# Moving part of an input projection and a compress chain beside attention units

## The reference

```python
mod = c @ w_ada[l] + b_ada[l]                    # six vectors of 1024
h = rms_norm(x, g_pre_mix[l]) * (1.0 + sc1[:, None]) + sh1[:, None]
proj = h @ w_in[l]                               # q_n, kc, vc, ks, vs, kw, vw, gates, q_d, k_d, v_d, qi, ki, wi
o_nsa = nsa_attention(rope(q_n), rope(kc), vc, rope(ksl), vsl, rope(kw), vw, ...)
o_dsa = dsa_attention(rope(q_d), rope(k_d), v_d, rope(qi), rope(ki), wi)
o = jnp.concatenate([o_nsa, o_dsa], axis=-1) @ w_out[l]
```

## Time and profile before

| what | us |
|---|---|
| median of 3 runs (lowest, highest) | 1342.13 (1339.54, 1344.83) |
| the profiled execution | 1338.55 |
| its span, first to last instruction | 1336.7 |
| first projection product | 25.75 |
| last projection product starts | 95.78 |
| scores of unit 0, 7 and 16 start | 100.23, 143.58, 185.76 |
| the heads' outputs are transposed | 222.75 |

### The profile page before, as it was taken

One profiled execution on the slowest core, in us unless ns is written; L12 is line 12 of the kernel. 1 busy time (PEld: TensorE's weight loads), 2 busy tenths in 40 slices (PEclk: granted clock), 3 DMA queues, 4 the chain that ended last, 5 costly groups with the idle time before them and its releaser, 6 DMA issues.

```text
span 1336.7 us, 13883 instructions
## 1 busy us (share of the span) xinstructions
PE 1147.5 (86%) x4788; PEld 748.5 (56%) x4788; DVE 846.1 (63%) x1810; ACT 478.0 (36%) x1042; POOL 555.8 (42%) x479
## 2 busy tenths in 40 slices
PE   6699899899999989999757797878978988877877
PEld 3577667699978689876623353433424434323332
DVE  5673578545453478665686767767677766777553
ACT  3453324556544566655212222122221222222211
POOL 2463632476676555413153343333433333334330
PEclk8896589999999999999978998888988889888998
DMA  9461243645476543222299999999999999999994
GB/s 386 188 215 37 91 143 114 248 158 183 164 272 225 177 146 127 95 79 95 90 423 422 420 422 421 422 420 422 420 422 421 421 421 421 422 421 421 422 421 167
DMA packets 53462, 381.15 MB, mean 285 GB/s; under 512 B 6160, under 2 KB 6544, under 8 KB 7568
## 3 DMA queue, kind: packets, MB, share of 16 engines
q0 software_dynamic: 36864, 268.45, 48.3%
q1 hardware_dynamic: 15664, 111.00, 23.0%
q10 hardware_dynamic: 864, 0.82, 0.2%
HBM read 379.20 MB, written 1.05 MB: 284 GB/s over the span
## 4 chain that ended last, share of the span: by engine, by line
PE 47%; DMA 33%; DVE 13%; ACT 3%; issue 3%; POOL 1%; PEldq 0%; PEld 0%; SPq 0%; DVEq 0%; POOLq 0%; ACTq 0%
DMA arena<-uv_dram,arena 22%; PE bank L766 14%; PE bank L1427 11%; PE row_bank L766 8%; PE bank L730 7%; DMA ring<-uv_dram,arena 5%; PE row_bank L730 3%; DMA ada<-uv_dram,arena 2%; DMA mix_rows<-uv_dram,arena 2%; DVE gain_rows_in L2767 2%; PE bank L1405 2%; POOL v_lo L1974 1%; DVE arena L2192 1%; PE bank L894 1%; DVE arena L2655 1%
## 5 line engine op out<-in xcount | busy, mean ns | idle before, releaser
L1427 PE MATMUL bank<-arena 128*128 128x512 f32 x684 | 338.3, 646 | 96.6 <-ACT arena L1895 96.2
L1974 POOL TENSOR_TENSOR v_lo<-ring,d_hi 128x512 fp32r<-128x512 f32 x189 | 267.1, 1427 | 260.6 <-ACT d_hi L1528 201.6
L1427 PEld LDWEIGHTS bank<-arena 128*128 128x128 f32 x684 | 137.8, 206 | 281.3 <-issue 161.5
L1962 POOL DMA_INDIRECT arena<-uv_dram,arena x171 | 161.5, 945 | 304.1 <-PE bank L1427 266.9
L1528 ACT CAST d_hi<-ring 128x512 fp32r<-128x512 f32 x204 | 123.5, 619 | 143.9 <-PE bank L766 85.6
L2767 DVE SCALAR_TENSOR_TENSOR gain_rows_in<-arena,row_bank 128x1024 f32<-128x1024 f32 x86 | 104.9, 1220 | 81.1 <-DMA arena<-uv_dram,arena 81.1
L1887 ACT ACTIVATE arena<-arena 128x4 f32<-128x4 f32 x64 | 13.1, 205 | 393.0 <-DVE gain_rows_in L2767 393.0
L2054 DVE TENSOR_TENSOR v_lo<-ring,d_hi 128x512 fp32r<-128x512 f32 x63 | 56.5, 897 | 140.1 <-ACT d_hi L1528 132.3
L2767 DVE SCALAR_TENSOR_TENSOR arena<-arena,row_bank 128x1024 f32<-128x1024 f32 x85 | 103.7, 1220 | 47.8 <-DMA arena<-uv_dram,arena 47.6
L1895 ACT ACTIVATE arena<-ident,arena 128x128 f32<-128x128 f32 x256 | 81.7, 389 | 108.3 <-DVE arena L2774 108.1
L730 PE MATMUL bank<-arena 128*128 128x128 f32 (+6 forms) x456 | 74.4, 320 | 9.5 <-DVE arena L2258 3.7
(11 more groups left out here) (390 smaller groups left out, 2270.1 us busy)
## 6 DMA issues: line engine op xcount, KB each, us to landing
ring<-w_dram SPq DMA_DIRECT2D x93, 1024.0 KB, 4.9
arena<-w_dram SPq DMA_DIRECT2D x9, 1024.0 KB, 11.2
arena<-uv_dram,arena POOLq DMA_INDIRECT x171, 24.2
x<-x_dram SPq DMA_DIRECT2D x1, 1024.0 KB, 5.5
arena<-mem_dram SPq DMA_DIRECT2D x1, 1024.0 KB, 17.5
out_dram<-x SPq DMA_DIRECT2D x2, 512.0 KB, 4.9
arena<-const_dram SPq DMA_DIRECT2D x1, 868.0 KB, 18.1
ring<-uv_dram,arena POOLq DMA_INDIRECT x34, 24.7
```

Of the source, the lines that this page charges most:

```text
L1427: last = nc.tensor.matmul(acc[tb, c][:, :], diag[:, s % N_DIAG, :], expert_rows(s)[:, D + c * 512:D + (c + 1) * 512], start=False, stop=(s ...
L1962: nc.gpsimd.indirect_dma_start(expert_rows(s), None, uv_in, bass.IndirectOffsetOnAxis(ap=ids[:, s:s + 1], axis=0)).then_inc(s_got[s % ROWS ...
L1974: nc.gpsimd.tensor_tensor(v_lo[:, r, :], dense_quarter(d, r), d_hi[:, r, :], ALU.subtract).then_inc(s_dpl, 1)
```

## The change

- Tile order: group 1 of `w_in` comes last (after 4), the two compress tiles come after the modulation tiles of 4 and 5 instead of before.
- Head: PE multiplies groups 0, 2, 3 (first halves), 0, 2, 3 (second halves), then 4. ACT splits ("in", 0, 1) ahead of the wait for the second gain, and the tile after it ahead of the memory's norm. DVE weighs both halves of early tile 3 before it splits the second tile. Group 1 is multiplied in PE's loops 1 to 4 (a quarter each) and 5 and 6 (two each); DVE rotates it in loops 7 and 8; its two `pairT` groups come in loop 9.
- All four index score products stand in loop 0 (before: loops 1 and 2). The compress chain moves from loops 0, 3, 4, 6, 7, 12, 13 to 12, 13, 14, 16, 17, 20, 21. The memory's transposes move from loops 20 to 23 to 24 and 25, their last two copies on DVE behind the units.
- `FILLED` goes from 11 loops to 18 (7 to 24); `WEIGH_UNITS`, `ROUNDS_AT`, `MOD_AT`, banks and some scratch buffers change.

```diff
-    tiles = [("in", n, k) for k in range(2) for n in range(3)]
-    tiles += [("in", n, k) for n in range(3, 5) for k in range(2)]
+    tiles = [("in", n, k) for k in range(2) for n in (0, 2, 3)]
+    tiles += [("in", n, k) for n in (4, 1) for k in range(2)]
+    tiles += [("ada", n, k) for k in range(2) for n in (4, 5)]
     tiles += [("cmp1", n, 0) for n in range(2)]
-    tiles += [("ada", n + m, k) for n in (4, 6) for k in range(2) for m in range(2)]
+    tiles += [("ada", n, k) for k in range(2) for n in (6, 7)]
...
-MOD_AT = {13: 5, 14: 4, 19: 6, 23: 7, 24: 8}
-WEIGH_UNITS = [2, 2, 5, 6, 7, 10, 11, 12, 12, 13, 13, 14, 15, 16, 16, 17, 17, 18, 19, 20, 20, 21, 21, 22]
+MOD_AT = {13: 4, 15: 5, 18: 6, 23: 7, 24: 8}
+WEIGH_UNITS = [0, 3, 4, 5, 6, 9, 9, 11, 11, 14, 14, 15, 15, 16, 16, 16, 20, 20, 20, 21, 21, 21, 22, 23]
...
-FILLED = (8, 9, 10, 11, 14, 15, 16, 17, 18, 19, 24)
-PAIR_GROUPS = ((0, 2), (5, 3), (1, 4), (6, 5), (4, 6), (2, 7), (3, 1))
-BESIDE = {0: ((("kcT",), 6), (("vcT",), 7)), 1: ((("L", 0), 6), (("L", 1), 7)), 2: ((("L", 2), 6), (("L", 3), 7)),
...
+FILLED = (0, *range(7, 25))
+PAIR_GROUPS = ((0, 0), (5, 1), (1, 2), (6, 3), (4, 6))
+BESIDE = {0: tuple((("L", n), (4, 5, 2, 3)[n]) for n in range(4)), 1: ((("in", 1, 0), 6), (("in", 1, 1), 7)),
+          9: ((("pairT", 2), 6), (("pairT", 3), 7)), 12: ((("kcT",), 4), (("vcT",), 5)),
+          13: ((("cmp", 0), 4),), 14: ((("cmp", 1), 5),), 16: ((("kcmp",), 4), (("vblk",), 5)),
+          17: ((("Sc", 0), 4), (("Sc", 1), 5)), 20: ((("pcT",), 6),), 21: ((("Oc", 0), 7), (("Oc", 1), 6)),
+          24: ((("memT", 0), 0), (("memT", 1), 1)), 25: ((("memT", 2), 6), (("memT", 3), 7))}
...
+                if 1 <= i < 5:
+                    in_quarter(1, 0, i - 1)
+                if i == 5 or i == 6:
+                    in_quarter(1, 1, 2 * (i - 5))
+                    in_quarter(1, 1, 2 * (i - 5) + 1)
+                if i == 9:
+                    pe.wait_ge(s_rot, 2)
+                    pair_features(2)
+                    pair_features(3)
+                if i == 12:
+                    compress_rows("kcT", rot, ROT_KC * HD)
+                    compress_rows("vcT", plain, PL_VC)
+                if i == 13 or i == 14:
+                    compress(i - 13)
...
             for q in range(2):
                 h1_high(q)
-            high_parts(("in", 2, 0))
+            high_parts(("in", 0, 1))
             act.wait_ge(s_gain, 2)
             for q in range(2, 4):
                 wait_read(act, ("h1T", q))
                 h1_high(q)
+            high_parts(("in", 2, 1))
             act.wait_ge(s_mem, 16)
             root(1, tmp)
...
             weigh_early(3, 0)
-            low_parts(("in", 1, 0))
             weigh_early(3, 1)
+            low_parts(("in", 2, 0))
             weigh_early(1, 0)
-            low_parts(("in", 2, 0))
+            low_parts(("in", 3, 0))
             weigh_early(1, 1)
...
+                j = i + 2
+                if j == 0:
+                    low_parts(("in", 1, 0))
...
+                if j == 5:
+                    low_parts(("in", 1, 1))
+                if j == 7:
+                    rotated(1, 0)
+                if j == 8:
+                    rotated(1, 1)
+                    nc.vector.memset(coef[:, 0:1], 0.0).then_inc(s_rot, 1)
+                if j == 12 or j == 13:
+                    compress_copied(j - 12)
```

More of the change, by code:

```diff
@@ L186, in psum_plan @@
     for tb in range(TB):
-        group(("in", 3, tb), 4 + tb)
-    for tb in range(TB):
-        group(("in", 4, tb), tb)
+        group(("in", 4, tb), 4 + tb)
     for n, bank in PAIR_GROUPS:
@@ L936, in _ @@
                 in_quarter(0, 0, r)
-            for n in range(1, 3):
+            for n in (2, 3):
                 for r in range(4):
@@ L941, in _, with pair_features @@
             ada_columns(1)
-            for n in range(3):
+            for n in (0, 2, 3):
                 for r in range(4):
                     in_quarter(n, 1, r)
[L945 to L948, removed]
+            for half in range(2):
+                for r in range(4):
+                    in_quarter(4, half, r)
             pe.wait_ge(s_const, 1)
             pe.wait_ge(s_rot, 1)
-            for n, _ in PAIR_GROUPS:
+            def pair_features(n):
                 ps = begin(("pairT", n))
@@ L964, in _ @@
                 end(last, ("pairT", n))
+            for n, _ in PAIR_GROUPS:
+                pair_features(n)
             def compress_rows(which, src, first):
@@ L1609, in _, with last_quarter @@
                 free(ins, ("pairT", n))
+            for n, _ in PAIR_GROUPS:
+                pair_copied(n)
+            high_parts(("in", 1, 0))
+            def last_quarter(r):
+                d = DENSE_AT[("in", 1, 1)]
+                wait_loaded(act, ("in", 1, 1))
+                act.wait_ge(s_dused, 4 * d + r - 3)
+                nc.scalar.copy(d_hi[:, r, :], dense_quarter(d, r)).then_inc(s_dhi, 1)
+                if r == 3:
+                    highs[0] += 1
             def hidden(which):
@@ L1630, in beside1 @@
             def beside1(i):
[L1632 to L1638, removed]
+                if i == 0:
+                    for n in range(4):
+                        index_relu(n)
+                if 2 <= i < 6:
+                    last_quarter(i - 2)
+                if i == 9:
+                    pair_copied(2)
+                    pair_copied(3)
@@ L1648, in beside1 @@
                     ps = wait_full(act, ("pcT",))
                     free(nc.scalar.copy(pcT.rearrange("p b t -> p (b t)"), ps[:, 0:T]), ("pcT",))
[L1650 to L1657, removed]
+                if i == 22:
+                    high_parts(("out", 0, 0))
@@ L1659, in _ @@
+                if i == 24:
+                    for q in range(2):
+                        ps = wait_full(act, ("memT", q))
+                        for kk in range(2):
+                            k = 2 * q + kk
+                            ins = nc.scalar.activation(memT[:, k, :], ps[:, kk * T:(kk + 1) * T], ACT.Copy,
+                                                       scale=vcol("memg", k))
+                        free(ins, ("memT", q))
             attention(UNITS1, lambda u, tb: KINDS[u[0]] + tb * HEADS + u[1], [(0, P), (P, P + T)], beside1)
-            wait_full(act, ("PT", *UNITS1[-1]))
@@ L2428, in _ @@
             low_parts(("out", 0, 0))
+            for q in range(2, 4):
+                ps = wait_full(dve, ("memT", q))
+                for kk in range(2):
+                    k = 2 * q + kk
+                    ins = ts(memT[:, k, :], ps[:, kk * T:(kk + 1) * T], vcol("memg", k), None, ALU.mult)
+                free(ins, ("memT", q))
             tt(gg[:, 0:8], mod[:, 16:24], vall("g_post_mix"), ALU.mult).then_inc(s_ggf, 1)
```

121 lines of the change are left out of this document (51 added, 70 removed).

## The result

| | median us (lowest, highest) | runs |
|---|---|---|
| before | 1341.31 (1339.03, 1344.83) | 5 |
| after | 1352.90 (1350.15, 1353.11) | 5 |

The ratio is 1.0072, with a 95% interval of 1.0057 to 1.0087: the change makes the kernel 11.6 us slower. 1328.5 was forecast, and 1339 was the upper end of the range.

A forecast was written before the change was run, and what follows sets the result against it. PE's order, with its low clock, was taken to bound the first 230 us. Terms -16.5 - 12.7 + 12.4 + 2.8 + 0.4 = -13.6 gave 1325.0 profiled, median 1328.5; range for 8 of 10: 1313 to 1339.

The forecast's parts named there:

- half of it at 0.5 costs +10 (4 to 20): Loops 12 to 15, behind the hole: half of about 20 us of full-clock work runs at half clock, +10 us.
- a low spell after the mask's wait or in unit 17: +3 (0 to 8): Unit 16 to the outputs' transposes: a low clock spell adds 3 us to the work.
- 36.8 of work: Unit 16 to the outputs' transposes: the units' work, mask wait included, sums to 36.8 us before any low clock.
- rival (b): Clock stays low from the hole in loop 12 on, through loop 17: +17 us, 1345.5; chance 0.15.
- no fillers then: Argument against the lasting low clock: the earlier low units up to 160 us had no fillers.
- nothing shows them keeping it high: Units 7 to 15: the compress products ran wholly at low clock before, with no evidence that they hold it high.
- Head, -16.5 forecast: Start to last projection product: two tiles gone -11.7, earlier resume -5.2, DVE's steps -0.6, norm +1.0.
- rival (c): Head: port contention with POOL holds DVE up fully, +2.1 us, 1330.6; chance 0.1.
- Last product to unit 7, -12.7 forecast: Last projection product to unit 7's scores: 35.1 us instead of 47.8, at full clock but 1.5 for one spell.
- The hole, 5.6 forecast: Loop 12, ahead of the compress rows: PE waits 5.6 us (3 to 7) because DVE's loop 11 awaits a load.
- The mask's wait, 1.1 forecast: Unit 16 to the transposes: PE waits 1.1 us for the dsa mask instead of 2.15.
- Behind, +0.4 forecast: Behind the units: DVE's memory copies and the outputs' split net +0.4 us (-1 to 1.5), the rest unchanged.

The follow-up runs named there:

- experiment 4: Experiment 2's second version with the last round of the top-64 search moved from DVE's loop 15 to 14: 1328.09 us, ratio 0.9897.
- experiment 3: Kernel before with its six fillers in every unit loop 1 to 24 instead of 11 loops: 1356.48 us, ratio 1.0110.
- experiment 1: Kernel after with block 0 of (ada, 6, 0) weighed in DVE's loop 14 instead of 11, removing the load wait: 1336.87 us, ratio 0.9965.
- experiment 2: Experiment 1 plus eight 256-column constant products inside each compress product; two versions, differing in the bank written: 1335.66 and 1335.10 us.
- experiment 6: Kernel before with eight constant products inside each of its two compress products (loops 3 and 4): 1335.39 us, ratio 0.9955.
- experiment 8: Two runs: kernel before with (in, 0, 1) and (in, 1, 1) split earlier, 1343.86 us; kernel after with the norm ahead of the second gain's wait, 1349.91 us.
- experiment 5: Kernel after with eight constant products inside each compress product, the load wait left in: 1343.53 us, ratio 1.0009.

## Why the prediction was wrong

**The step that failed is the clock's, twice.** "About 20 us of full-clock work follow in loops 12 to 15; half of it at 0.5 costs +10 (4 to 20)", and "a low spell after the mask's wait or in unit 17: +3 (0 to 8)". Measured: units 7 to 15 took 64.6 us in the kernel after, and 45.7 in experiment 4 (115.70 to 161.43), which has a hole 5.6 us shorter, 16 constant products of 1.0 us together, and a low spell of 3.4 us of its own, which cost 1.7; 64.6 - 45.7 - 5.6 + 1.0 + 1.7 = 16.0 us of clock. From unit 16 on 50.8 us against the forecast's 36.8 of work: 14 us, which is half of the 28.6 us that the clock was still low there. Together about 30, where 13 were forecast, and beyond the 26.6 from which rival (b) decided. Rival (b), at 0.15 of the chance and 1345.5, was nearest: it had the length and the compress products, but not the whole course. The clock did not stay low from the hole on, it came back at 148.1 and fell again inside the first compress product, and the stretch lasted through unit 19 rather than 17.

The reason I gave against (b) was "no fillers then". Experiment 3 shows what it was worth: with fillers in all loops the clock was low for 48 us all the same. I had read the 0.99 of 160 to 185.76 as the work of the fillers and the 0.59 in front of it as the lack of them, but the rows between them differ in a second thing, the narrow products, and I had priced these myself ("nothing shows them keeping it high") and drew no length from it. The only stretch of the trace before that had compress products in it was low to its end, 160, and windows cut finer show that it began inside the first of them, at 116.1 (so the prediction's "ran wholly at the low clock" misses 1.5 us); that, not half of 20 us, was the nearest row.

**Head, -16.5 forecast, -12.7 measured.** The two tiles went as said. PE resumes at 54.36, not at about 52: rival (c), at its full price. DVE's timeline of the kernel after, and POOL's beside it:

```profile
44.06 5.03 DVE L2220 SCALAR_TENSOR_TENSOR arena<-arena 128x512 f32<-128x512 f32 x4
```

```profile
42.30 4.67 POOL L2002 TENSOR_TENSOR v_lo<-ring,d_hi 128x512 fp32r<-128x512 f32 x3 [0.45 <-ACT d_hi L1539]
```

Four steps take 5.0 us in place of 4 x 0.76 = 3.0; those begun while POOL subtracts take 1.7. That is 2.0 us on the path to the gain. The Trainium skill's rule (SBUF — State Buffer, section "Who interferes with whom") agrees with these rows. The norm behind the second tile cost 2.0 us of waits (0.93 + 0.17 + 0.45 + 0.44), not 1.0.

**Last product to unit 7, -12.7 forecast, -14.5 measured.** Right in mechanism and nearly in size: the quarter tiles beside the units run at 1.00, and the 1.5 us for a low spell weren't needed.

**The hole, 5.6 forecast, 6.94 measured.** Place, releaser and chain as forecast, the load's wait 5.10 where 5.0 stood. That taking it away gave 16 us (experiment 1), and not its 5.6, is the clock. Of the +10.0 in units 7 to 15 the clock is 6.0 and the hole 1.3; the remaining 2.7 lie in work I had summed too tightly, 0.7 of it the compress products (3.74 us each at the full clock, not 3.4).

**The mask's wait, 1.1 forecast, 0.17 measured:** at half the clock PE comes late enough. In experiment 2, at full clock, it was 2.05. A wait can hide behind the very slowness it would cause.

**Behind, +0.4 forecast, +5.4 measured.** The outputs' first product follows the transposes by 3.7 us (before 3.6), so the tail edit is right. Laid beside each other from there on, the two traces part at three places above all: the kernel after loses 1.3 us in the FFN's products 43 us behind the transposes, 1.5 us at 396, and 1.7 us in the last 12 us. At each it has a low spell of 3.4 us that the kernel before hasn't. The windows of the first two places, after and then before:

```profile
274.00:278.00 4.00, 4.00 (x24) 4.00 (x23) 3.90 (x8) 1.04 (x2) 1.29 (x1) 0.57 0.18 74
629.00:633.00 4.00, 4.00 (x13) 3.09 (x12) 0.81 (x2) 0.62 (x1) 1.28 (x1) 0.57 0.39 164
```

```profile
265.00:269.00 4.00, 4.00 (x35) 4.00 (x35) 3.90 (x8) 1.64 (x3) 1.92 (x2) 1.00 0.15 61
619.00:623.00 4.00, 4.00 (x19) 3.30 (x18) 0.63 (x2) 1.48 (x3) 2.18 (x2) 1.00 0.36 152
```

So 4.5 of the 5.4 us are the clock again, at a place where the prediction let nothing change. Part of it is the yardstick: the profiled execution before, 1338.55, is 2.8 us under its median. All profiled kernels with the new order have 1120.1 to 1121.4 us behind the transposes, the edited ones with the old order 1118.5 to 1118.9, and only the kernel before 1115.8. Why the new order keeps some 2 us more stays open.

**What the reordering itself is worth.** With filled compress products and a wait for the mask in both, the old order takes 1335.4 (experiment 6) and the new one, without the load's wait, 1335.1 (experiment 2): the same. The 1328.1 of experiment 4 has the mask's round moved as well, which no run tried in the old order. The new order's lead is 19.7 us at unit 7 (115.83 against 135.56) and 2.6 at the transposes (213.74 against 216.35): most of it was work and low clock that only moved behind unit 7.

**That experiment 4 comes out at the forecast** (1328.1, forecast 1328.5) is luck: it has no mask wait and a hole of 1.35 us where 5.6 were forecast, and its low stretch lies elsewhere.

## What to carry to other kernels

Price a low clock by the longest stretch that the trace shows with the same kind of work in it, not by what a short wait was followed by: dense-looking loops with 45- and 15-column products between small transposes lost it for 41 to 58 us, in the kernel after with PE 98% busy. When a tile order changes, walk through every slot of the load ring again: two blocks of tiles n and n+4 in one loop are a load's latency on the engine that weighs them. Compare orders with the same waits taken out of both. And measure such kernels in many runs and read the mean clock of each, for one and the same program gave 1326.7 and 1346.0 us, another 1323.1 and 1332.6.

## What the runs showed of the hardware

The granted clock can fall with no hole of PE right ahead: in experiment 1 at 145.2 among the products of 45 columns, with PE busy 2.05 of 2.05 us ahead of them and no hole since 137.2. One constant product of 256 columns before every four of 45 went with 1.00 through both compress products in seven of eight profiled runs; without constants the clock fell inside a compress product in four of six (before, after, experiments 1 and 3), at the end of one in the fifth and ahead of it in the sixth (both in experiment 8). Six such products in a row once per loop did not hold it (experiment 3). What ends a low stretch no run tells: it came back after 17 to 58 us among units like those in which it had stayed low.

A hole of 6.8 us needn't cost much clock: in experiment 5 it was back at 1.00 within 5.5 us of its end. The Trainium skill (TensorE: Matmul & The Clock Gate, section "HAM oscillation — how this bites in real kernels") has idle gaps bring the clock down, waits for DMA of some 3 to 5 us in its example. Experiments 2, 5 and 6 agree that a hole brings it down, but by shorter ones: there the clock is low from 0 to 0.9 us behind the end of waits of 2.05, 2.14 and 1.20 us on. Experiment 1, and the second fall of experiment 6, are falls that the section doesn't cover.
